# Products of constants in TensorE's waits, and a sparse attention whose side work is spread over more blocks

## The chip, the cores and the metric

The kernel runs on one core of a Trainium2 chip. The metric is the device time of one launch in microseconds (us). TensorE (PE) does the matrix products, VectorE (DVE) and ScalarE (ACT) the elementwise work, GpSimd (POOL) a few fills and loads, and SyncE issues most DMAs.

## The reference

The network has 256 tokens of width 1024, all in fp32. Two "hybrid" layers come first, then a pooling mixer with a gated network, then a sparse attention with a mixture of eight experts. Cut to what matters here:

```python
for layer in range(2):                      # hybrid layers
    h = rms_norm(x, norm1_g)
    mq, mk, mv, mo, mi, mf, aq, ak, av = split(h @ w_in)
    y = concat([mlstm(mq, mk, mv, mi, mf) * sigmoid(mo), dilated_attention(aq, ak, av)])
    x = x + y @ w_out
    x = x + relu(rms_norm(x, norm2_g) @ w_up) ** 2 @ w_down
x = rms_norm(x, final_g)
x = layer_norm(ALPHA * x + pool_mixer(x));  x = layer_norm(ALPHA * x + swiglu(x))
q, kc, vc, ks, vs, kw, vw, gates = split(x @ nsa_w_in)
kc, vc = compress(kc), compress(vc)         # silu(blocks @ w1) @ w2, 15 blocks of keys
o = g0 * attend(q, kc, vc) + g1 * attend(q, ks, vs) + g2 * attend(q, kw, vw)
x = layer_norm(ALPHA * x + o @ nsa_w_out);  x = layer_norm(ALPHA * x + moe_ffn(x))
```

## The kernel before

The tokens stand in two tiles of 128 rows. A weight matrix comes in units of 128 x 2048 through a ring of buffers. ScalarE copies each unit to `HI` in a rounded format (`split_hi`, L495), VectorE forms the rest `LO` (`split_lo`, L503), and TensorE makes every product of a weight as three products (L513), so that it keeps the precision of fp32. Activations are split in the same way after they are transposed: `turn_rows` (L671) transposes a tile of rows on TensorE into a PSUM bank, `cols_hi` (L678) and `cols_lo` (L686) write the two halves `XTH` and `XTL`, and only then can the products of that tile begin. `cols_by_tile` makes all products of tile 0 first, turns tile 1 between, and then makes those of tile 1.

Each engine runs one list of instructions in program order, and semaphores (`filled`, `a_bank`, `v_bank`, `a_done`, `v_done`) order them against one another. The `Banks` class deals out PSUM: four banks in turn with `take`, four named ones (`BA`) with `hold`. Whoever takes a bank waits until its last user's content has been read by ScalarE or VectorE.

In a hybrid layer `scores_tensor` (L1227) and `spread_sums_tensor` (L1214) belong to the mLSTM; `ml_turn_tensor` (L1238) and `ml_gather_tensor` (L1251) transpose its weights and multiply them by the values. The attention loops (`attention_tensor`, `attention_scalar`, `attention_vector`) run over blocks n of two heads: TensorE makes the scores of block n (`att_weigh`, L795), VectorE masks them and takes the maximum (L812, L816), ScalarE takes the exponential (L824), TensorE transposes the weights of block n-3 (`att_turn`, L833), ScalarE evicts them (L842), and TensorE multiplies those of block n-4 by the values (`att_gather`, L858). The dilated attention has 8 blocks, the sparse one 32 (two kinds of keys, two tiles, eight pairs of heads). `mid` is a table of extra steps: {n: work} runs that work in block n of the loop.

In the sparse attention the extra steps hold the whole branch of compressed keys: `blocks_tensor` (L1813) and `sparse_keys_tensor` (L1822) come before the loop; in the loop are `compress_tensor` (L1837) and `compress2_tensor` (L1850), the copy of the compressed values (`values_c_vector`, L2063), `weigh_c` (scores, softmax without its division: L1866, L2079 to L2088, ScalarE L2006), `turn_c` (division and transposition: L2093 to L2102, L1874, ScalarE L2011) and `gather_c` (product by the values and sum into `NY`: L1883, L2115, L2122). `sparse_heads` (L2129 to L2144) scales a finished tile of heads and adds it to `NY`.

`route_tensor` (L2274) counts the tokens of each expert, and `fetch_tensor` (L2295) gathers the rows of the first expert.

## Time and profile before

| | |
|---|---|
| median of 3 runs | 2351.45 us (2349.92 to 2353.35) |
| the profiled execution | 2355.53 us, of which the trace spans 2353.7 us |
| mean granted clock of TensorE | 0.958 of full speed |
| busy: TensorE, VectorE, ScalarE, GpSimd | 91%, 68%, 56%, 1% of the span |

The profile has one execution. A row of a timeline gives start and duration in us, the engine, the source line, what is written and read, the count, and in brackets how long the engine sat idle just before and whose instruction ended that wait.
### The profile page before, as it was taken

The page shows a single profiled execution, that of the slowest core. Times are in us where ns is not written, and L with a number is a line of the kernel's source. Part 1 is how long each engine was busy: PE and PEld are TensorE (multiplying, and loading weights), DVE is VectorE, ACT ScalarE, POOL GpSimd, SP SyncE. Part 2 cuts the span into 40 slices and gives each one's busy share as a digit, 9 for nine tenths or more (in the row PEclk, how much of TensorE's full clock was granted, in tenths as well). Part 3 has the DMA queues.
Part 4 walks back from the last instruction along what each step waited for, and adds up shares of the span by engine and source line. Part 5 has one row for each costly group of instructions (what it writes and reads, how often), then busy time and mean ns, then how long its engine had stood idle before and what let it go on. Part 6 is the DMA issues. An engine that isn't in the chain of part 4 may idle for free.

```text
span 2353.7 us, 25771 instructions
## 1 busy us (share of the span) xinstructions
PE 2137.2 (91%) x9918; PEld 1723.0 (73%) x9918; DVE 1596.9 (68%) x1540; ACT 1321.6 (56%) x1374; POOL 22.1 (1%) x33
## 2 busy tenths in 40 slices
PE   6888999978999799988777999999999989898986
PEld 5666887767788588777565888788888866666665
DVE  3865555775555554565655555788888889898997
ACT  4554444644444344445543444577776778787876
POOL 0000000000000000000000000000000000000000
PEclk9989999988999899997897999999999999999999
DMA  6313543431654254532005555688998999898995
GB/s 238 150 45 136 190 179 129 161 114 54 234 185 181 96 197 180 178 138 83 0 1 210 221 214 189 239 346 344 336 368 335 357 351 412 350 414 346 412 375 219
DMA packets 74336, 524.26 MB, mean 223 GB/s; under 512 B 8705, under 2 KB 9153, under 8 KB 11873
## 3 DMA queue, kind: packets, MB, share of 16 engines
q1 hardware_dynamic: 71424, 511.64, 56.7%
q0 software_dynamic: 2784, 10.93, 1.3%
q8 instruction: 80, 1.31, 0.2%
q14 instruction: 48, 0.39, 0.0%
HBM read 521.48 MB, written 1.05 MB: 222 GB/s over the span
## 4 chain that ended last, share of the span: by engine, by line
PE 71%; DVE 15%; ACT 8%; issue 5%; DMA 0%; DVEq 0%; ACTq 0%; SPq 0%
PE psum L513 52%; PE psum L523 8%; DVE LO L503 6%; ACT HI L495 3%; PE psum L1004 3%; DVE AR L1475 1%; PE psum L2295 1%; PE psum L1009 1%; PE psum L795 1%; PE psum L2323 1%; PE psum L858 1%; DVE XT L686 1%; ACT AR L824 1%; PE psum L671 1%; PE psum L1837 1%
## 5 line engine op out<-in xcount | busy, mean ns | idle before, releaser
L503 DVE TENSOR_TENSOR LO<-ring,HI 128x2048 fp32r<-128x2048 f32 x379 | 851.3, 2258 | 425.9 <-ACT HI L495 424.0
L495 ACT ACTIVATE HI<-ring 128x2048 fp32r<-128x2048 f32 x379 | 712.7, 1886 | 344.4 <-PE psum L513 282.5
L513 PE MATMUL psum<-HI,XT 128*128 128x512 f32 (+1 forms) x2592 | 842.4, 400 | 61.2 <-DVE XT L686 30.2
L513 PEld LDWEIGHTS psum<-HI,XT 128*128 128x128 f32 x2592 | 503.4, 195 | 178.8 <-DVE XT L686 34.2
L513 PE MATMUL psum<-LO,XT 128*128 128x512 f32 (+1 forms) x1296 | 514.3, 397 | 0.0
L513 PEld LDWEIGHTS psum<-LO,XT 128*128 128x128 f32 x1296 | 253.5, 196 | 50.5
L503 DVE TENSOR_TENSOR LO<-AR,HI 128x2048 fp32r<-128x2048 f32 x112 | 254.3, 2289 | 48.3 <-ACT HI L495 47.8
L523 PE MATMUL psum<-HI,XT 128*128 128x512 f32 x560 | 231.2, 413 | 39.8 <-DVE LO L503 38.4
L495 ACT ACTIVATE HI<-AR 128x2048 fp32r<-128x2048 f32 x112 | 213.4, 1911 | 61.7 <-PE psum L523 37.6
L513 PE MATMUL psum<-HI,HTH 128*128 128x512 f32 x568 | 225.1, 396 | 0.0
L513 PE MATMUL psum<-HI,HTL 128*128 128x512 f32 x568 | 221.6, 390 | 0.0
L513 PE MATMUL psum<-LO,HTH 128*128 128x512 f32 x568 | 221.2, 389 | 0.0
L523 PE MATMUL psum<-LO,XT 128*128 128x512 f32 x560 | 220.6, 394 | 0.0
L523 PEld LDWEIGHTS psum<-HI,XT 128*128 128x128 f32 x560 | 105.6, 188 | 99.4 <-issue 40.8
L967 ACT ACTIVATE AR<-psum 128x512 f32<-128x512 f32 (+1 forms) x107 | 63.5, 593 | 112.1 <-PE psum L513 93.1
L513 PEld LDWEIGHTS psum<-HI,HTL 128*128 128x128 f32 x568 | 106.6, 188 | 22.7
L513 PEld LDWEIGHTS psum<-LO,HTH 128*128 128x128 f32 x568 | 106.8, 188 | 21.0
L513 PEld LDWEIGHTS psum<-HI,HTH 128*128 128x128 f32 x568 | 106.7, 188 | 20.8
L523 PEld LDWEIGHTS psum<-LO,XT 128*128 128x128 f32 x560 | 105.8, 189 | 20.7 <-issue 1.0
L523 PE MATMUL psum<-HI,HTH 128*128 128x512 f32 x280 | 112.6, 402 | 5.0 <-DVE HTH L1061 4.6
L523 PE MATMUL psum<-LO,HTH 128*128 128x512 f32 x280 | 109.5, 391 | 0.0
L1025 ACT ACTIVATE HTH<-psum 128x512 fp32r<-128x512 f32 (+1 forms) x72 | 42.7, 593 | 57.4 <-PE psum L1009 52.8
(272 smaller groups left out, 1826.7 us busy)
## 6 DMA issues: line engine op xcount, KB each, us to landing
ring<-in_experts SPq DMA_DIRECT2D x224, 1024.0 KB, 6.8
ring<-in_dense SPq DMA_DIRECT2D x149, 1024.0 KB, 4.8
AR<-in_experts SPq DMA_DIRECT2D x112, 1024.0 KB, 6.8
bcs<-in_ln_g POOLq DMA_DIRECT2D x4, 512.0 KB, 4.5
bcs<-in_ln_b POOLq DMA_DIRECT2D x4, 512.0 KB, 5.0
bcs<-in_norm_g POOLq DMA_DIRECT2D x3, 512.0 KB, 4.0
cons<-in_cons POOLq DMA_DIRECT2D x1, 1317.0 KB, 8.1
X<-in_x SPq DMA_DIRECT2D x2, 512.0 KB, 4.1
```

Source lines behind the costliest of these rows:

```text
L495: e.activation(HI[:, h:h + m], slot(u), ACT.Copy).then_inc(*high.up(u))
L503: e.tensor_tensor(LO[:, h:h + m], slot(u), HI[:, h:h + m].bitcast(F32), ALU.subtract).then_inc(*low.up(u))
L513: ins = e.matmul(out_ap, lhsT=a, rhs=b, start=start and n == 0, stop=stop and n == m - 1)
L523: ins = e.matmul(out_ap, lhsT=both, rhs=b, start=start and n == 0, stop=stop and n == m - 1)
L671: ins = e.transpose(bank[:, j * P:(j + 1) * P], src(k0 + j), ident)
L686: e.tensor_tensor(XTL[:, k0:k0 + 4, tile(t)], banks.get(name, "cols", t, k0).rearrange("p (k s) -> p k s", k=4), XTH[:, k0:k0 + 4, tile(t) ...
L795: e.matmul(bank[:, 0:2 * nk], lhsT=a.qT[:, b, tile(qt)], rhs=a.kz(kind, b)[:, :, 0:nk], start=True, stop=True).then_inc(*filled.up(a.name, ...
L824: e.activation(w3[:, h, :], w3[:, h, :], ACT.Exp, bias=nm[:, h:h + 1], accum_out=l[:, 2 * b + h:2 * b + h + 1]).then_inc(*a_done.up(a.name ...
L858: ins = e.matmul(bank[:, col:col + 64], lhsT=a.PT2[:, n % 2, tile(h * kt + i)], rhs=a.v(kind, i, head), start=i == 0, stop=i == kt - 1)
L967: e.activation(GS[:, hb, t, 0:n], banks.get(use, "up", c, t)[:, 0:n], f).then_inc(*a_bank.up(use, "up", c, t))
L1004: ins = e.matmul(bank[:, o:o + PACK], lhsT=src[:, tile(j)], rhs=C("pairs"), start=True, stop=True)
L1025: e.activation(HTH[:, hb, 0:nb, tile(t)], bank[:, 0:n].rearrange("p (j s) -> p j s", j=nb), ACT.Copy).then_inc(*a_done.up(use, "turn", c, t))
```

## The change

A new function `idle` multiplies the identity matrix by 512 columns of constants, into the PSUM bank that is next in turn or a named one, and nobody reads the result. A bank that was last used so need not be waited for. There are 51 such products of 128x512, between the steps of TensorE's program: before or after transpositions (`wait`, `rest` of `turn_rows`), before `scores_tensor` and before the products of `av`, in blocks 2, 7 and 9 of the dilated attention, four at the start of the pooling, five between the transpositions of `blocks_tensor`, one before the queries of the sparse attention are transposed, and around the routing. `idle_first` makes 10, 18 and 4 products of 128x128 at the start of the first layer, when only the identity matrix is loaded. In the sparse attention the steps `turn_c`, `gather_c` and `weigh_c` of TensorE, ScalarE and VectorE move to later and different blocks; the sum over the weights (L2088) moves from `weigh_c` to the start of `turn_c`; the copy of the compressed values goes ahead of a `split_lo` in VectorE's list; the result of `compress2_tensor` goes to a named bank; and the turning and splitting of output tile 0 moves into the last blocks of the loop. The diff, cut to its core (ScalarE's table of steps changes in the same way: `weigh_c` to blocks 13 and 20, `turn_c` to 16 and 23):

```diff
     def hold(self, e, b, *use):
         before = self.use.get(b)
-        if before is not None:
+        if before is not None and before[0] != "idle":
...
+    def next(self, e, *use):
+        return self.hold(e, self.n % 4, *use)
...
-        def turn_rows(e, name, t, src, ready):
+        def idle(e, n, b=None):
+            if n:
+                bank = banks.next(e, "idle") if b is None else banks.hold(e, b, "idle")
+                e.wait_ge(s_cons, 16)
+                for _ in range(n):
+                    e.matmul(bank, lhsT=ident, rhs=cons[:, 0:512], start=True, stop=True)
+
+        def idle_first(e, n):
+            bank = banks.hold(e, BA[0], "idle")
+            e.wait_ge(s_ident, 16)
+            for _ in range(n):
+                e.matmul(bank[:, 0:P], lhsT=ident, rhs=ident, start=True, stop=True)
+
+        def turn_rows(e, name, t, src, ready, wait=0, rest=1, b=None):
+            idle(e, wait, b)
             for k0 in range(0, KB, 4):
...
+            idle(e, rest, b)
...
+            if l == 0:
+                idle_first(e, 10)
+            turn_rows(e, n1, 0, lambda k: ROWS[:, 0, tile(k)], rows_at(n1, 0), rest=l)
+            if l == 0:
+                idle_first(e, 18)
+            def second_rows():
+                turn_rows(e, n1, 1, lambda k: ROWS[:, 1, tile(k)], rows_at(n1, 1), wait=l, rest=l, b=BA[0])
+                if l == 0:
+                    idle_first(e, 4)
...
+            idle(e, 1)
             scores_tensor(e, l)
...
             spread_sums_tensor(e, l, 1)
+            idle(e, 1)
             cols(e, ("av", l), ("av", l), BOTH, xr, mid={0: lambda: ml_turn_tensor(e, l, 1),
...
-            attention_tensor(e, dilated(l), {1: lambda: ml_turn_tensor(e, l, 3),
-                                             2: lambda: ml_gather_tensor(e, l, 3)})
+            def gather_last():
+                idle(e, 1)
+                ml_gather_tensor(e, l, 3)
+            steps = {1: lambda: ml_turn_tensor(e, l, 3), 2: gather_last, 7: lambda: idle(e, 1),
+                     9: lambda: idle(e, 1)}
+            attention_tensor(e, dilated(l), steps)
...
         def pool_tensor(e):
+            idle(e, 4)
...
-            turn_rows(e, "l0", 0, lambda k: X[:, 0, tile(k)], [v_done.of("l0", "rows", 0)])
+            turn_rows(e, "l0", 0, lambda k: X[:, 0, tile(k)], [v_done.of("l0", "rows", 0)], wait=1,
+                      rest=3)
...
         def blocks_tensor(e, kind):
             for gp in range(2):
+                idle(e, 1 if kind or gp else 2)
...
-            bank = banks.take(e, "cmp", kind)
+            bank = banks.hold(e, BA[3 - kind], "cmp", kind)
...
-                     6: lambda: weigh_c_tensor(e, 0), 7: lambda: turn_c_tensor(e, 0),
-                     8: lambda: gather_c_tensor(e, 0), 9: lambda: weigh_c_tensor(e, 1),
-                     10: lambda: turn_c_tensor(e, 1), 11: lambda: gather_c_tensor(e, 1)}
-            attention_tensor(e, SPARSE, {2 * n: f for n, f in steps.items()})
+                     6: lambda: weigh_c_tensor(e, 0)}
+            steps = {2 * n: f for n, f in steps.items()}
+            steps |= {16: lambda: turn_c_tensor(e, 0), 18: lambda: gather_c_tensor(e, 0),
+                      19: lambda: weigh_c_tensor(e, 1), 23: lambda: turn_c_tensor(e, 1),
+                      25: lambda: gather_c_tensor(e, 1), 33: lambda: y_tile(0)}
...
-            y_tile(0)
+            attention_tensor(e, SPARSE, steps)
             project_out_tensor(e, ("po", 2), "out2", x_ready("y.2"), lambda: y_tile(1))
...
         def turn_c_vector(e, qt):
             l, gl, W = sm(16, "c_l"), sm(16, "c_gl"), WC[:, qt, :]
+            e.wait_ge(*a_done.of("wc", qt))
+            e.wait_ge(*v_order.last)
+            e.tensor_reduce(l, W.rearrange("p (h k) -> p h k", h=16), AX.X,
+                            ALU.add).then_inc(*v_done.up())
...
-                     4: lambda: hidden_vector(e, 1), 5: lambda: [split_lo(e), values_c_vector(e)],
+                     4: lambda: hidden_vector(e, 1), 5: lambda: [values_c_vector(e), split_lo(e)]}
...
+            steps |= {12: lambda: weigh_c_vector(e, 0), 14: lambda: turn_c_vector(e, 0),
+                      18: lambda: gather_c_vector(e, 0), 19: lambda: weigh_c_vector(e, 1),
+                      21: lambda: turn_c_vector(e, 1), 25: lambda: gather_c_vector(e, 1),
+                      34: lambda: cols_lo(e, "y.2", 0)}
...
         def route_tensor(e):
+            idle(e, 1)
...
-            turn_rows(e, "l2", 1, lambda k: X[:, 1, tile(k)], [v_done.of("l2", "rows", 1)])
+            turn_rows(e, "l2", 1, lambda k: X[:, 1, tile(k)], [v_done.of("l2", "rows", 1)], wait=4)
...
             route_tensor(e)
+            idle(e, 2)
```

How the lists of instructions change in three places. In the kernel of before, TensorE at the end of the dilated attention of layer 0 (from block 7's scores, L795, to the transposition of tile 0 of the output, L671):

```order
L795 MATMUL psum<-AR 128x512
L833 MATMUL psum<-cons,AR 128x128 x4
L858 MATMUL psum<-AR 128x64 x4
L833 MATMUL psum<-cons,AR 128x128 x4
L858 MATMUL psum<-AR 128x64 x4
L833 MATMUL psum<-cons,AR 128x128 x4
L858 MATMUL psum<-AR 128x64 x4
L833 MATMUL psum<-cons,AR 128x128 x4
L858 MATMUL psum<-AR 128x64 x8
L671 MATMUL psum<-cons,AR 128x128 x8
```

In the changed kernel, whose lines have moved (L818 is scores, L856 transposition, L881 the product by the values, L693 the output's transposition, L675 the product of constants):

```order
L818 MATMUL psum<-AR 128x512
L675 MATMUL psum<-cons 128x512
L856 MATMUL psum<-cons,AR 128x128 x4
L881 MATMUL psum<-AR 128x64 x4
L856 MATMUL psum<-cons,AR 128x128 x4
L881 MATMUL psum<-AR 128x64 x4
L675 MATMUL psum<-cons 128x512
L856 MATMUL psum<-cons,AR 128x128 x4
L881 MATMUL psum<-AR 128x64 x4
L856 MATMUL psum<-cons,AR 128x128 x4
L881 MATMUL psum<-AR 128x64 x8
L693 MATMUL psum<-cons,AR 128x128 x8
L675 MATMUL psum<-cons 128x512
```

Three products of constants stand in this stretch, two in the loop and one behind the output's transposition.

TensorE in blocks 14 to 18 of the sparse attention, before (L1874 is `turn_c`, L1883 `gather_c`):

```order
L795 MATMUL psum<-AR 128x512
L1874 MATMUL psum<-cons,AR 128x128 x4
L833 MATMUL psum<-cons,AR 128x128 x4
L858 MATMUL psum<-AR 128x64 x4
L795 MATMUL psum<-AR 128x512
L833 MATMUL psum<-cons,AR 128x128 x4
L858 MATMUL psum<-AR 128x64 x4
L795 MATMUL psum<-AR 128x256
L1883 MATMUL psum<-AR 128x256 x4
L833 MATMUL psum<-cons,AR 128x128 x4
L858 MATMUL psum<-AR 128x64 x4
L795 MATMUL psum<-AR 128x256
```

and in the changed kernel in blocks 16 to 19 (L1914 is `turn_c`, L1923 `gather_c`):

```order
L818 MATMUL psum<-AR 128x256
L1914 MATMUL psum<-cons,AR 128x128 x4
L856 MATMUL psum<-cons,AR 128x128 x4
L881 MATMUL psum<-AR 128x64 x4
L818 MATMUL psum<-AR 128x256
L856 MATMUL psum<-cons,AR 128x128 x4
L881 MATMUL psum<-AR 128x64 x4
L818 MATMUL psum<-AR 128x256
L1923 MATMUL psum<-AR 128x256 x4
L856 MATMUL psum<-cons,AR 128x128 x4
L881 MATMUL psum<-AR 128x64 x4
L818 MATMUL psum<-AR 128x256
```

`turn_c` stood in block 14 and stands in block 16; `gather_c` went from block 16 to block 18.

VectorE around `weigh_c` of tile 0, before (L2079 to L2088 is `weigh_c`, L2093 to L2102 `turn_c`):

```order
L2079 SCALAR_TENSOR_TENSOR AR<-psum,cons 128x512
L2083 TENSOR_REDUCE SML<-AR 128x16
L2085 TENSOR_TENSOR AR<-AR,SML 128x512
L2088 TENSOR_REDUCE SML<-AR 128x16
L812 SCALAR_TENSOR_TENSOR AR<-psum,cons 128x512
L816 TENSOR_REDUCE SML<-AR 128x2
L812 SCALAR_TENSOR_TENSOR AR<-psum,cons 128x512
L816 TENSOR_REDUCE SML<-AR 128x2
L2093 RECIPROCAL SML<-SML 128x16
L2096 SCALAR_TENSOR_TENSOR SML<-SML,cons,AR 128x16
L2102 COPY AR<-AR 128x4x4x32
```

and in the changed kernel (L2122 to L2128 is `weigh_c`, L2134 to L2146 `turn_c`, L835 and L839 the mask and maximum of a block):

```order
L2122 SCALAR_TENSOR_TENSOR AR<-psum,cons 128x512
L2126 TENSOR_REDUCE SML<-AR 128x16
L2128 TENSOR_TENSOR AR<-AR,SML 128x512
L835 SCALAR_TENSOR_TENSOR AR<-psum,cons 128x512
L839 TENSOR_REDUCE SML<-AR 128x2
L835 SCALAR_TENSOR_TENSOR AR<-psum,cons 128x512
L839 TENSOR_REDUCE SML<-AR 128x2
L2134 TENSOR_REDUCE SML<-AR 128x16
L2137 RECIPROCAL SML<-SML 128x16
L2140 SCALAR_TENSOR_TENSOR SML<-SML,cons,AR 128x16
L2146 COPY AR<-AR 128x4x4x32
```

The sum over the weights, which needs ScalarE's exponential, no longer follows directly behind the subtraction: two blocks' masks stand between.

## Rows read from the trace of the kernel before

**Rows 1.** The page: TensorE's granted clock in 40 slices

```profile
PEclk9989999988999899997897999999999999999999
```

**Rows 2.** Stretches of the span: length, busy us of PE, PEld, DVE, ACT, POOL, granted clock, DMA

```profile
0.00:1290.00 1290.00, 1136.58 (x5303) 928.55 (x5304) 739.08 (x983) 586.37 (x799) 22.13 (x33) 0.93 0.38 139
115.50:123.00 7.50, 5.59 (x14) 4.41 (x15) 5.29 (x9) 1.86 (x4) 0.00 (x0) 0.54 0.17 69
167.00:181.00 14.00, 12.54 (x48) 11.15 (x49) 4.20 (x8) 2.38 (x4) 0.44 (x1) 0.51 0.11 37
1075.00:1113.00 38.00, 33.54 (x141) 29.45 (x141) 19.45 (x48) 23.69 (x57) 0.00 (x0) 0.55 0.19 68
1127.20:1176.30 49.10, 37.18 (x205) 31.15 (x206) 34.51 (x69) 21.95 (x66) 0.00 (x0) 0.80 0.00 1
1235.00:1263.00 28.00, 15.11 (x73) 12.23 (x74) 13.01 (x43) 5.62 (x11) 2.80 (x3) 0.57 0.29 108
```

**Rows 3.** TensorE's timeline, tile 1 of the first projection

```profile
29.30 0.50 PE L513 MATMUL psum<-HI,XT 128*128 128x512 f32 x1 [1.77 <-DVE XT L686]
...
29.87 0.63 PE L513 MATMUL psum<-HI,XT 128*128 128x512 f32 x2
...
30.57 0.98 PE L513 MATMUL psum<-HI,XT 128*128 128x512 f32 x2
```

**Rows 4.** TensorE's timeline, one fp32 product of 128x512 at either clock

```profile
1138.07 2.02 PE L795 MATMUL psum<-AR 128*128 128x512 f32 x2
1139.88 0.65 PE L833 MATMUL psum<-cons,AR 128*128 128x128 f32 x4
...
1146.58 1.08 PE L795 MATMUL psum<-AR 128*128 128x512 f32 x2
1147.50 0.60 PE L833 MATMUL psum<-cons,AR 128*128 128x128 f32 x4
```

**Rows 5.** TensorE's timeline, from scores to spread sums, in layer 0 and 1

```profile
98.12 1.13 PE L1227 MATMUL psum<-AR 128*128 128x256 f32 x4 [1.31 <-DVE AR L908]
...
113.48 1.99 PE L1214 MATMUL psum<-AR,cons 8*128 8x256 f32 x8 [1.97 <-DVE AR L1568]
...
475.18 2.08 PE L1227 MATMUL psum<-AR 128*128 128x256 f32 x4 [1.31 <-DVE AR L908]
...
492.24 1.99 PE L1214 MATMUL psum<-AR,cons 8*128 8x256 f32 x8 [0.78 <-DVE AR L1568]
```

**Rows 6.** TensorE's timeline, waits at which the change puts something

```profile
18.43 0.77 PE L513 MATMUL psum<-HI,XT 128*128 128x512 f32 x1 [6.99 <-DVE LO L503]
...
117.41 0.77 PE L513 MATMUL psum<-HI,XT 128*128 128x512 f32 x1 [1.95 <-DVE AR L908]
...
166.95 1.80 PE L858 MATMUL psum<-AR 128*128 128x64 f32 x8 [2.53 <-ACT AR L842]
...
176.08 0.77 PE L513 MATMUL psum<-HI,XT 128*128 128x512 f32 x1 [1.46 <-DVE XT L686]
...
781.61 8.81 PE L1708 MATMUL psum<-AR,X 128*128 128x256 f32 x32 [5.93 <-DVE X L717]
...
1130.44 2.08 PE L795 MATMUL psum<-AR 128*128 128x512 f32 x2 [5.69 <-DVE AR L2063]
...
1144.81 0.66 PE L1874 MATMUL psum<-cons,AR 128*128 128x128 f32 x4 [2.53 <-DVE AR L2102]
...
1165.11 1.11 PE L1874 MATMUL psum<-cons,AR 128*128 128x128 f32 x4 [5.38 <-DVE AR L2102]
...
1204.14 0.47 PE L513 MATMUL psum<-HI,XT 128*128 128x512 f32 x1 [4.22 <-DVE XT L686]
...
1240.03 1.97 PE L671 MATMUL psum<-cons,X 128*128 128x128 f32 x8 [7.50 <-DVE X L752]
```

**Rows 7.** VectorE's timeline, first low half of the blocks, and copies of compressed values

```profile
1073.50 0.40 DVE L2034 TENSOR_TENSOR XT<-psum,XT 64x240 fp32r<-64x240 f32 x1 [1.31 <-ACT XT L1938]
...
1129.41 0.98 DVE L2063 COPY AR<-psum 32x64 f32<-32x64 f32 x4
```

39 lines of the change are left out of this document (17 added, 22 removed).

## The prediction

> **What bounds the kernel now.** I read the page first. TensorE is busy 91% of the span (table above), and the slices of its granted clock are not all 9: in the first half some are 8 and two are 7 [rows 1]. So I took the two halves of the span apart [rows 2]. Up to 1290 us the granted clock averages 0.93. The clock has two levels, 1.2 and 2.4 GHz, so a mean of 0.93 means that about 2 x 0.07 x 1290 = 180 us ran at the lower one. TensorE was busy in 1136.58 of those 1290 us, 88%, hence some 158 us of work ran at half speed, and no change of the clock alone can give back more than half of that, 79 us. The experts' half of the kernel (behind 1290 us) gets none of the change and is left at nothing.
>
> The timeline shows what the engine did before the clock fell. In tile 1 of the first projection TensorE turned a tile, then waited 1.77 us for VectorE's low half (L686), and soon its products come slower: a pair on `HI` takes 0.63 us at 29.87 and 0.98 at 30.57 [rows 3]. The same work at either level is in [rows 4]: the scores of a block of the sparse attention take 1139.88 - 1138.07 = 1.81 us from start to start at the low clock and 1147.50 - 1146.58 = 0.92 us at the full one. This is an fp32 product of 128x512, just what the change adds, so 0.92 and 1.81 us are the prices of one added product. A product of 128x128 I take at a quarter, 0.23 and 0.46 us (an estimate from the two).
>
> What one short stretch at the low clock costs is seen where both layers do the same work. From the wait before the third scores to the spread sums it takes 113.48 - 98.12 = 15.36 us in layer 0, where the clock stays up, and 492.24 - 475.18 = 17.06 us in layer 1, where it falls [rows 5]. So one such stretch costs 1.7 us, though waits on VectorE lie behind it.
>
> **Where the added products lie.** Each place must have a wait that covers 0.92 us. They are in [rows 6]: 6.99 us before the first product, 1.95 us before `av`, 2.53 us in the last blocks of the dilated attention, 1.46 and (elsewhere, as in rows 3) 1.77 us behind a turned tile, 5.93 us before the pooling, and 7.50 us before tile 1 of the experts' input. 51 products of 0.92 us are 47 us of work, and I cost what lies in these waits at nothing. The cover is gone where the product itself runs at the low clock: 1.81 us no longer fits in 1.77 or 1.46 us. The bank of an added product is the one that the next step takes, or one already read, so its wait is one that TensorE would have made anyway.
>
> **The terms.** (1) Dilated attention, both layers. The wait of 2.53 us before the product at 166.95 ends with ScalarE's L842, which the added products don't touch: the two of blocks 7 and 9, 1.84 us, fit in it. What follows at 167 to 181 us ran wholly at the low clock (0.51), with 12.54 us of busy TensorE [rows 2]; at full clock that is 6.3 us less. The wait for L686 at 176.08 stays and may grow by half a us, so 5.8 us, twice: 11.6.
> (2) Before `av`. The stretch 115.5 to 123 has 5.59 busy us at 0.54 [rows 2]; half is 2.8, of which I take 2.3, since a later wait on ScalarE takes some. Twice: 4.6.
> (3) Layer 1's scores: 1.7 [rows 5].
> (4) Tile 1 of five projections and networks, each with a stretch as in rows 3: 1.7 each, less where the next wait (on an eviction) takes some: 7.7.
> (5) Pooling: its products start at 781.61 behind 5.93 us of waiting [rows 6], where four added ones are 3.7 us; the network's first tile follows behind a like wait. A stretch each, the second with less work in it: 1.7 + 1.5 = 3.2.
> (6) Start: at 18.43 the first product records 0.77 us, as slow as the one at 176.08, against 0.50 us for a first product at full clock [rows 3, 6]. The start gains between nothing and one and a half stretches, 2.5 us; the ten products before the first transposition are 4.6 us at the low clock, begin only when the identity has landed, and may delay it by 1.1. I take 1.4.
> (7) Routing: 1235 to 1263 us is at a low clock, with 15.11 busy us [rows 2]. Half would be 7.5; the chain runs through many small VectorE steps and a DMA, so I take 4. Four products and one more lie in the 7.50 us of waiting.
> (8) Sparse attention. TensorE waits 5.69 us at 1130.44 behind the copies L2063, 2.53 at 1144.81 and 5.38 at 1165.11 behind `turn_c` of VectorE [rows 6]. With `turn_c` two blocks later on TensorE than on VectorE the last two should go. Of the first only the copy itself, 0.98 us [rows 7], goes, since VectorE's `split_lo` still waits for ScalarE's half of the unit. That is 2.53 + 5.38 + 0.98 = 8.9. Upper bound: in 1127.2 to 1176.3 VectorE is busy 34.51 of 49.10 us [rows 2], so 14.6 is all that there is before it becomes the bound; lower bound nothing, if the waits only move. At the end, the first product of the output waits 4.22 us (1204.14) behind VectorE's last heads and the splitting of tile 0 [rows 6]. With tile 0 turned and split inside the loop that wait nearly goes, 4.1, and the fall of the clock at 1204.7 with it, 1.7. Against that, two products (1.84 us) now stand ahead of the first transposition of `blocks_tensor`. ScalarE and then VectorE (L2034, which starts at 1073.50 behind ScalarE [rows 7]; its half of the tensors of one kind is eight such instructions) work their way from it to the first mask with hardly a pause, so this costs 1.4. Sum: 8.9 + 5.8 - 1.4 = 13.3. That the clock stays up in the compressing products, 1075 to 1113 us [rows 2], I do not assume: TensorE's waits on L2034 are longer than what is put into them.
>
> Two more places I cost at nothing. The product before the last gather of the mLSTM stands behind the wait that lets the clock fall, so it runs low (1.81 us, only partly covered) and may help the clock back. The one before the queries of the sparse attention is followed by a wait for ScalarE that takes it up.
>
> Sum: 11.6 + 4.6 + 1.7 + 7.7 + 3.2 + 1.4 + 4 + 13.3 = 47.5. Where the clock falls depends on moments that shift when everything before gets shorter, so some stretch will remain: I take off 4, which leaves 43.5 us. The profiled execution took 2355.5 us, 4 above the median of 2351.45; the differences are taken from the median: 2351.45 - 43.5 = 2308 us.
>
> **A rule of the Trainium skill.** At 29.30 us a wait of 1.77 us comes just before a fall of the clock [rows 3]. The Trainium skill, "TensorE: Matmul & The Clock Gate", in "Why this matters for your kernels", names only pauses clearly longer than that one as what makes the clock drop. By that rule terms 1 to 4 would give nothing; by the row they give. The trace speaks against the rule here.
>
> **Rivals.** A: only long waits matter, and filling the short ones changes nothing, as there something else pulls the clock down, for instance the transpositions around them. Then terms 1 to 4 go and 5 to 8 stay: 3.2 + 1.4 + 4 + 13.3 = 21.9, or 2329.5 us. For it: the stretch at 1075 us is low with TensorE 88% busy [rows 2], so more than waiting counts. Against it: rows 3 and 5. The rule above would end here too. Chance 0.15.
> B: the clock holds, but the spreading of the sparse attention gives nothing, since VectorE has as much to do and its two long pieces (`gather_c`, heads) now meet around block 19. Then 13.3 becomes -1.4: 47.5 - 14.7 - 4 = 28.8, or 2322.6 us. For it: VectorE is at 70% there. Chance 0.15.
> C: the clock also holds through the compressing products: 33.54 busy us at 0.55 are up to 15 us more, of which 12: 2296 us. Chance 0.10.
> D, slower: the clock doesn't respond, and the products run low. Of the 51, some 25 stand ahead of a step that another engine waits for (scores, last gather, dilated attention, blocks, pooling, routing); at 1.81 us each that is 45 us, of which waits cover about half, so 23 us are added against 10 from the spreading: 2351.45 + 13 = 2364 us. It decides once uncovered time is more than what clock and spreading give back. Rows 3 speak against it. Chance 0.05.
> E: gains and costs cancel, within 0.2%: 0.03.
>
> **How the numbers follow.** The forecast has 0.52, with 2299 to 2317 as its own range. The range of all reaches down to 2290, past C, and up to 2332, past A and B; D and the far ends are outside, under 0.2 together. 0.2% of the time is about what a measurement of this kernel can tell from no change. Every case but D and E is faster: 0.92, same 0.03, slower 0.05.
>
> **What would show each step.** The mean clock up to 1290 us should rise from 0.93 to about 0.97. In the two stretches behind the dilated attention it should be near 1 and the wait before L842's reader about 0.7 us instead of 2.53 (1). Layer 1 should take the same 15.4 us as layer 0 (3). The product behind the sparse attention should wait under 1 us instead of 4.22, and TensorE's waits behind `turn_c` be gone (8); if VectorE's idle time in the loop stays while TensorE waits on its masks instead, B is right. `blocks_tensor` should finish some 3.5 us later on TensorE, and L2034 start 1.4 us later. What would make me wrong above all: a clock that falls at new places as often as it stays up at the old ones.

## The result, and the profile after

The changed kernel takes 2323.91 us, the median of 4 runs (2321.12 to 2327.8), against 2351.09 us of the kernel before (4 runs): the ratio is 0.9883, with a 95% interval of 0.9869 to 0.9897. 27.2 us were gained where 43.5 were forecast. The time lies in the whole range (2290 to 2332), but outside the forecast's own 2299 to 2317; of the cases priced it is nearest to rival B's 2322.6, whose mechanism (the spreading gives nothing) the runs below refute. The profiled execution spans 2326.0 us, 27.7 less than the 2353.7 us of before.

The page of the changed kernel (busy us, share of the span and instructions; granted clock in 40 slices):

```profile
PE 2166.2 (93%) x10084; PEld 1729.2 (74%) x10084; DVE 1597.3 (69%) x1540; ACT 1322.1 (57%) x1374; POOL 22.2 (1%) x33
...
PEclk9989999999999999997898999999999999999999
```

TensorE is busy 29.0 us more than before, though the span is 27.7 us shorter: it waits less, and what fills the waits is no work of the network. Of the four 8s that [rows 1] has in its first sixteen slices three have become 9s; around the middle the 7s and 8s are still there but for one 7.

Stretches of the changed kernel (columns as in [rows 2]); the first and the last answer to the first and the fourth of [rows 2]:

```profile
0.00:1261.00 1261.00, 1163.66 (x5470) 932.88 (x5471) 739.32 (x983) 586.85 (x799) 22.20 (x33) 0.96 0.38 143
111.00:118.00 7.00, 7.00 (x16) 4.41 (x15) 6.48 (x12) 0.02 (x1) 0.00 (x0) 0.51 0.36 143
163.00:173.00 10.00, 8.98 (x42) 7.49 (x43) 5.23 (x9) 3.26 (x6) 0.54 (x1) 0.66 0.14 54
1066.00:1098.00 32.00, 29.47 (x130) 26.74 (x129) 15.27 (x37) 19.77 (x46) 0.00 (x0) 0.57 0.19 67
```

Up to the experts the granted clock is 0.96 where it was 0.93; 2 x 0.04 x 1261 = 101 us ran at the lower level, against some 180. The compressing products (1066 to 1098) still run low for 2 x 0.43 x 32 = 28 us, where 2 x 0.45 x 38 = 34 us were low before. The places at 111 and at 163 us, ahead of `av` and at the end of the dilated attention, are still low too, though products of constants stand in both.

To see where the 27.7 us came from, the start of the same VectorE instruction was read in the timelines of both profiles; how much the distance to the start above it has shrunk is what that stretch gained. The starts, and the terms of the prediction (in us):

```
the stretch ends at (in brackets the term)     before    changed  gained  forecast
splitting of tile 1, first projection (6)        27.76     26.28    1.48    1.4
after tile 1 of that projection (4)              39.12     36.03    1.61
dilated attention, past av, last gather (2)     154.47    151.54   -0.16    2.3
end of the dilated attention (1)                185.12    178.97    3.22    5.8
after tile 1 of layer 0's network (4)           416.19    408.77    1.27
layer 1's scores (3)                            491.49    482.40    1.67    1.7
dilated attention, past av, last gather (2)     533.31    524.03    0.19    2.3
end of the dilated attention (1)                563.94    551.43    3.23    5.8
two projections' tile 1 (4)                     604.77    589.02    3.24
pooling, tile 1 of its network (5)              814.14    800.61   -2.22    3.2
tile 1 of the queries (4; 7.7 for its five)    1019.63   1004.45    1.65    7.7
blocks of the compressed keys, L2034 (8)       1073.50   1059.65   -1.33   -1.4
mask behind the copies L2063 (8)               1130.49   1114.54    2.10    1.0
loop, to the last heads (8)                    1199.08   1179.67    3.46    7.9
tail, to the output's tile 1 (8)               1212.58   1187.76    5.41    5.8
routing and first gather (7)                   1276.56   1246.44    5.30    4.0
end of the span                                2353.7    2326.0    -2.42    0
taken off for stretches that remain                                        -4
sum                                                                27.70   43.5
```

Terms 3, 4, 6, the blocks and the tail fit within half a us. That is a fit of one profile to one profile; which of these gains are the products' is read below, in two more. At the scores of layer 1 the distance of [rows 5] is now 483.14 - 467.78 = 15.36 us, what layer 0 had (TensorE's timeline):

```profile
467.78 1.13 PE L1250 MATMUL psum<-AR 128*128 128x256 f32 x4 [1.31 <-DVE AR L931]
...
483.14 3.31 PE L1237 MATMUL psum<-AR,cons 8*128 8x256 f32 x7 [1.94 <-DVE AR L1605]
```

The misses are four: term 1, term 2, term 5 and the loop in term 8.

### The profile page after: what moved, and what is told of

Same layout as the page of the kernel before. It is cut to its first block, busy times and chain, and to the rows that moved or that the text cites. A ratio compares the mean times of both kernels' runs of the same rounds, so it can differ in the third digit from the quotient of the medians.

```text
span 2326.0 us, 26094 instructions
## 1 busy us (share of the span) xinstructions
PE 2166.2 (93%) x10084; PEld 1729.2 (74%) x10084; DVE 1597.3 (69%) x1540; ACT 1322.1 (57%) x1374; POOL 22.2 (1%) x33
## 3 DMA queue, kind: packets, MB, share of 16 engines
HBM read 521.48 MB, written 1.05 MB: 225 GB/s over the span
## 4 chain that ended last, share of the span: by engine, by line
PE 72%; DVE 15%; ACT 8%; issue 5%; DMA 0%; DVEq 0%; ACTq 0%; POOLq 0%
PE psum L517 51%; PE psum L527 9%; DVE LO L507 6%; ACT HI L499 3%; PE psum L1027 3%; DVE AR L1512 1%; PE psum L1032 1%; PE psum L2340 1%; PE psum L2368 1%; PE psum L675 1%; PE psum L881 1%; PE psum L818 1%; DVE XT L709 1%; ACT AR L847 1%; PE psum L1877 1%
## 5 line engine op out<-in xcount | busy, mean ns | idle before, releaser
L517 PE MATMUL psum<-HI,XT 128*128 128x512 f32 (+1 forms) x2592 | 828.6, 394 | 33.5 <-DVE XT L709 11.8
L517 PEld LDWEIGHTS psum<-HI,XT 128*128 128x128 f32 x2592 | 493.0, 191 | 156.7 <-DVE XT L709 24.5
L517 PE MATMUL psum<-LO,XT 128*128 128x512 f32 (+1 forms) x1296 | 505.8, 390 | 0.0
L527 PEld LDWEIGHTS psum<-HI,XT 128*128 128x128 f32 x560 | 106.6, 190 | 98.1 <-issue 40.3
```

The lines of the kernel that those rows point to most:

```text
L517: ins = e.matmul(out_ap, lhsT=a, rhs=b, start=start and n == 0, stop=stop and n == m - 1)
L527: ins = e.matmul(out_ap, lhsT=both, rhs=b, start=start and n == 0, stop=stop and n == m - 1)
```

## The experiments

The times are medians of 4 to 6 runs (one run for `changed_again`), and each median has its ratio to runs of the kernel before on the same chip. A ratio is uncertain by 0.12 to 0.23%, 3 to 5 us, so what is smaller is read in the profiles; and a profile is one execution, whose stretches at the low clock are its own.

**The two halves of the change.** `constants_only` has all products of constants and the old tables of steps; `spread_only` has the new tables and in `idle` and `idle_first` no product.

> This kernel has all the products of constants, and the sparse attention as it was before (steps in the old blocks, output tile 0 transposed behind the loop). Theory: constants and spreading act apart. In the two profiles VectorE's instructions of the sparse attention's loop gain 4.4 us and the turning of the output's tile 0 another 5.4 us, some 10 of the 27 us; the rest, 17 us, is the constants', so about 2334 us. Rival: the spreading's gain comes mostly from the clock that the constants hold, and alone the constants give more: 2328 us or less. Second rival: the spreading is most of the change, as the constants' own cost eats their gain: 2342 us or more.

> This kernel has the sparse attention as in the changed kernel and no product of constants. Theory: spreading gives 10 us, so about 2341 us, and its stretches at the low clock ahead of the sparse attention are those of the kernel before. Rival (the two need each other): no faster than 2346 us, since the clock falls in the loop where TensorE waits. The other side: the spreading alone gives 15 us or more (2336 us), as forecast from the waits behind the steps (8.9 and 5.8 us).

Measured: 2333.82 us (0.9927, 0.9913 to 0.9940) and 2340.59 us (0.9955, 0.9942 to 0.9969). Against 2351.0 these are gains of 17.2 and 10.4 us, 27.6 together, where the whole change gives 27.2. Within what these medians can tell the halves act apart, and the first theory holds in both runs; rival B (the spreading gives nothing) is out.

**Are the short waits worth anything?**

```diff
-        def turn_rows(e, name, t, src, ready, wait=0, rest=1, b=None):
+        def turn_rows(e, name, t, src, ready, wait=0, rest=0, b=None):
...
-            idle(e, 1)
             scores_tensor(e, l)
...
-             7: lambda: idle(e, 1), 9: lambda: idle(e, 1)}
```

> The changed kernel without 30 of the 51 products of constants and without the last four of the start: those around every transposed tile of rows, before the scores, before the product of av, before the last gather and in blocks 7 and 9 of the dilated attention, where TensorE waits 2.6 us at most. Those in long waits (pooling, blocks, routing, start) and the spread sparse attention stay. Theory: the short waits are worth most of what the constants give: 7.8 us at tile 1 of five places, 6.5 us at the ends of the dilated attention, 1.7 us at layer 1's scores, 16 us, so about 2340 us. Rival A of the prediction (only long waits matter): 2324 us, no change.

Measured: 2339.34 us (0.9955, 0.9942 to 0.9969), 15.4 us slower than the changed kernel. Rival A (only long waits matter) is out. The end of the dilated attention is again what it was in [rows 6], waits and slow product alike (TensorE's timeline of this kernel):

```profile
163.74 1.93 PE L881 MATMUL psum<-AR 128*128 128x64 f32 x8 [2.53 <-ACT AR L865]
...
173.00 0.77 PE L517 MATMUL psum<-HI,XT 128*128 128x512 f32 x1 [1.46 <-DVE XT L709]
```

**One kernel, two profiles.** The changed kernel was profiled once more.

> The changed kernel once more, for a second profile of the same instructions. Theory: which stretches run at the low clock differs from one execution to the next, so the ends of the two dilated attentions, which ran low for 6.8 us each in the first profile and for none in that of the kernel with the constants alone, may be low or not; the span lies between 2318 and 2327 us. Rival: the low stretches are fixed by the program, and stand at the same instructions as in the first profile.

Measured: 2324.05 us, span 2322.2. Stretches of the second profile, the ends of both dilated attentions:

```profile
165.50:172.50 7.00, 7.00 (x33) 6.70 (x33) 2.92 (x6) 1.59 (x3) 0.00 (x0) 0.51 0.22 75
535.00:548.00 13.00, 10.45 (x63) 8.44 (x62) 6.56 (x11) 4.62 (x8) 0.00 (x0) 1.00 0.01 2
```

and the second end in the first profile:

```profile
537.00:545.50 8.50, 8.50 (x40) 7.08 (x40) 3.86 (x7) 1.94 (x4) 0.00 (x0) 0.60 0.00 1
```

Layer 0's end is low in both; layer 1's was at 0.60 in the first and is at 1.00 in the second. The theory holds: the same instructions run at either level from one execution to the next. Over the ten profiles of kernels with these products, 14 of the 20 ends are low for 6.8 us and 6 not at all. In the three kernels without them there (before, `spread_only`, `no_short_waits`) all six ends are low for 13.7 us.

The starts that gave the table of gains were read in this second profile too, and in that of `spread_only`, which up to the sparse attention has the instructions of the kernel before and no product of constants. Gains against the profile of before, in us:

```
the stretch ends at                     changed   changed again   spread_only
splitting of tile 1, first projection      1.48        0.40           0.60
after tile 1 of that projection            1.61        1.60           1.62
layer 0: past av, last gather             -0.16        0.12          -1.24
layer 0: end of the dilated attention      3.22        2.65           0.02
after tile 1 of layer 0's network          1.27        1.32          -1.58
layer 1's scores                           1.67        1.17           1.67
layer 1: past av, last gather              0.19        1.12          -0.01
layer 1: end of the dilated attention      3.23        5.31           0.00
two projections' tile 1                    3.24        3.23           3.23
pooling, tile 1 of its network            -2.22        0.37           0.10
tile 1 of the queries                      1.65        1.59          -0.03
```

Two things follow. One place's gain differs by up to 2.6 us between two executions of the same kernel (pooling). And at three places `spread_only` gains as much without any product: 1.62 in the first projection, 1.67 at layer 1's scores, 3.23 at layer 1's two projections, 6.5 us in all. `no_short_waits` agrees, with no product ahead of the scores and 488.89 - 473.54 = 15.35 us from them to the sums:

```profile
473.54 1.13 PE L1250 MATMUL psum<-AR 128*128 128x256 f32 x4 [1.31 <-DVE AR L931]
...
488.89 1.99 PE L1237 MATMUL psum<-AR,cons 8*128 8x256 f32 x8 [1.94 <-DVE AR L1599]
```

A stretch of `spread_only` over the two projections:

```profile
560.00:610.00 50.00, 42.51 (x194) 33.93 (x193) 28.93 (x30) 23.52 (x27) 3.01 (x5) 1.00 0.58 209
```

So the profile of before had low stretches there that other executions without the products don't have, and its 6.5 us aren't shown to be the products' gain. What the two profiles do show as theirs is tile 1 of layer 0's network (2.9 us against `spread_only`), tile 1 of the queries (1.6 to 1.7) and the ends of the dilated attention (2.6 to 3.2 us where they run low, 5.3 where they don't).

**A bank that isn't empty: the pooling.** The place where the changed kernel lost in its first profile. Its TensorE, from the products ahead of the pooling to the network's first:

```profile
759.78 3.59 PE L675 MATMUL psum<-cons 128*128 128x512 f32 x8
...
765.88 8.83 PE L1746 MATMUL psum<-AR,X 128*128 128x256 f32 x32 [2.50 <-DVE X L740]
...
784.95 1.09 PE L693 MATMUL psum<-cons,X 128*128 128x128 f32 x8 [1.41 <-DVE X L775]
...
788.61 5.42 PE L675 MATMUL psum<-cons 128*128 128x512 f32 x6 [2.57 <-DVE AR L1795]
...
793.11 1.15 PE L517 MATMUL psum<-HI,XT 128*128 128x512 f32 x1
```

The same first product in the kernel before:

```profile
805.95 0.77 PE L513 MATMUL psum<-HI,XT 128*128 128x512 f32 x1 [4.14 <-DVE AR L1756]
```

and VectorE in the changed kernel, the reading of the pooled tile 1:

```profile
787.86 0.69 DVE L1795 TENSOR_TENSOR AR<-psum,AR 128x512 f32<-128x512 f32 x1
```

The three products behind the transposition (L675, x6) could start at 786.0, but wait 2.57 us for L1795, since the bank next in turn holds the pooled tile 1. They then run at the low clock, and the network's first product comes at 793.11: 27.23 us behind the first pooling product, where before it was 805.95 - 781.61 = 24.34 [rows 6].

```diff
-            turn_rows(e, "l0", 0, ..., wait=1, rest=3)
+            turn_rows(e, "l0", 0, ..., wait=1, rest=3, b=BA[0])
```

> The changed kernel, but the four products of constants around the pooled tile 0 are written to a named bank that is empty instead of the bank next in turn. Theory: in the changed kernel the three behind the transposition wait for VectorE's read of the pooled tile 1 (they start at 788.6 us, 2.57 us late) and then run at the low clock, so that the network's first product starts 3 us after its own bank came free; in the empty bank they start as soon as the transposition ends, and that product starts 2.5 to 3.5 us earlier, 2321 us in all. Rival: the bank is not what holds it, the product waits for VectorE's chain as in the kernel before, and the change of bank moves the start of the first product by less than 1 us.

```profile
764.13 8.83 PE L1746 MATMUL psum<-AR,X 128*128 128x256 f32 x32 [2.50 <-DVE X L740]
...
784.19 2.74 PE L675 MATMUL psum<-cons 128*128 128x512 f32 x6
...
788.50 0.47 PE L517 MATMUL psum<-HI,XT 128*128 128x512 f32 x1 [1.57 <-DVE AR L1795]
```

Now the three start at 784.19 as soon as the transposition ends, and the first product comes 788.50 - 764.13 = 24.37 us behind the pooling's: the 2.9 us are back, and the stretch at the low clock in the network (787 to 794 us) is gone as well. From VectorE's reading of the pooled tile 1 (L1795) to its next splitting (L709) it takes 3.6 us less. The theory holds. The median, 2323.29 us (0.9882, 0.9867 to 0.9898), hardly shows it; the profiled execution is the fastest of the four (2319.24).

The clock has a part in the 2.9 us. The changed kernel's second profile has the same wait of 2.57 us:

```profile
764.69 7.14 PE L1746 MATMUL psum<-AR,X 128*128 128x256 f32 x32 [2.50 <-DVE X L740]
...
785.73 4.52 PE L675 MATMUL psum<-cons 128*128 128x512 f32 x6 [2.57 <-DVE AR L1795]
```

but its first pooling products take 7.14 us where they took 8.83, and the network's first product comes 789.27 - 764.69 = 24.58 us behind them. With the 1.69 us of the pooling products set aside, the wrong bank costs 24.58 - (24.37 - 1.69) = 1.9 us there, and 2.9 in the first profile. Of the nine profiles with the bank next in turn four have 27.2 us, one 26.1 and four 24.5 to 24.7.

**Ahead of `av`.** In the first profile of the changed kernel the clock falls just behind the wait ahead of layer 0's spread sums (at 111.2 us), before the added product is reached, so that it runs low itself (TensorE's timeline):

```profile
110.41 3.07 PE L1237 MATMUL psum<-AR,cons 8*128 8x256 f32 x8 [1.94 <-DVE AR L1605]
...
113.41 2.08 PE L675 MATMUL psum<-cons 128*128 128x512 f32 x2
```

Two kernels put one product more ahead of the sums:

```diff
+            idle(e, 1)             # av_before_sums: bank next in turn
+            idle(e, 1, BA[0])      # av_empty_bank: a bank read long before
             spread_sums_tensor(e, l, 1)
             idle(e, 1)
```

> The changed kernel with one product of constants more in each layer, ahead of the spread sums of the second pair of heads, where TensorE waits 1.94 us. Theory: the clock falls there because of the wait ahead of the sums, and the product that the change has put behind the sums comes too late; with one in that wait too, the stretch at the low clock at 111 to 118 us goes in both layers, and this place gains 1.5 to 2.5 us each, 2320 us in all. Rival (the clock isn't ruled by single waits): a low stretch of the same length stays within 10 us of the place, and the time stays at 2324 us or grows by the uncovered part, about 1 us.

Measured: 2337.63 us (0.9937, 0.9923 to 0.9950), 13.7 us slower than the changed kernel. Neither theory nor rival had that. The profile shows the larger part of why: the bank next in turn is still read by L931, so the product waits 3.38 us where the sums waited 1.94, and the sums begin at 114.07 and no longer at 110.41:

```profile
112.06 2.07 PE L675 MATMUL psum<-cons 128*128 128x512 f32 x2 [3.38 <-DVE AR L931]
...
114.07 3.78 PE L1237 MATMUL psum<-AR,cons 8*128 8x256 f32 x8
```

By VectorE's starts the two places lose 3.9 and 2.7 of the 9.9 us by which this profile is longer than the changed kernel's first. Another 2.6 go at the tail of the sparse attention, where the clock falls at 1186.7 us; no run shows what brings that about.

> As the earlier run with a product ahead of the spread sums, but into a named bank that has been read long before (in the earlier run the product waited 3.38 us for a bank that VectorE's L931 read, where the sums alone waited 1.94 us). Theory: now it lies in the wait, the clock stays up at 111 to 118 us, and each layer gains 1 to 2 us: 2321 us. Rival: the clock falls there for other reasons (the small sums and transpositions around it), and the time stays within 1.5 us of 2324 us.

```profile
113.64 1.02 PE L675 MATMUL psum<-cons 128*128 128x512 f32 x2
...
114.60 1.99 PE L1237 MATMUL psum<-AR,cons 8*128 8x256 f32 x8
...
116.51 1.13 PE L675 MATMUL psum<-cons 128*128 128x512 f32 x2
...
118.48 0.50 PE L517 MATMUL psum<-HI,XT 128*128 128x512 f32 x1 [0.84 <-DVE AR L931]
```

Measured: 2320.18 us (0.9865, 0.9850 to 0.9880), 3.7 us below the changed kernel, with intervals that overlap. In this layer there is no wait ahead of the product or the sums, all run at the full clock, and the first product of `av` takes 0.50 us. But here an earlier low stretch (96.8 to 103.6 us) had made TensorE late. In layer 1 of the same profile a wait of 1.08 us is left, and the clock falls for 3.4 us behind the sums:

```profile
481.82 1.99 PE L1237 MATMUL psum<-AR,cons 8*128 8x256 f32 x8 [1.08 <-DVE AR L1606]
```

In the three profiles with this product (here, `three_banks`, `block9_twice`) the stretch past `av` gains 1.4 to 1.6 us in layer 0, where the seven of kernels with the other products and without this one gain -0.2 to 0.2. In layer 1 the scores and the stretch past `av` together gain 2.2 us in all three and 1.9 to 3.2 in the seven, so nothing is shown there. The product in the read bank is worth about 1.6 us, then, and the rest of the 3.7 isn't shown to be its own; in the wrong bank it costs 13.7.

**The end of the sparse attention.** Of the loop and the tail, VectorE and TensorE of the changed kernel:

```profile
1138.79 0.69 DVE L2122 SCALAR_TENSOR_TENSOR AR<-psum,cons 128x512 f32<-128x512 f32 x1
...
1141.54 1.42 DVE L2181 TENSOR_TENSOR AR<-psum,SML 128x512 f32<-128x512 f32 x2
...
1143.06 0.42 DVE L835 SCALAR_TENSOR_TENSOR AR<-psum,cons 128x256 f32<-128x256 f32 x1
...
1180.17 0.69 DVE L2181 TENSOR_TENSOR AR<-psum,SML 128x512 f32<-128x512 f32 x1
```

```profile
1143.54 0.70 PE L818 MATMUL psum<-AR 128*128 128x256 f32 x2 [2.07 <-DVE AR L835]
...
1146.18 1.11 PE L881 MATMUL psum<-AR 128*128 128x64 f32 x4 [1.73 <-ACT AR L865]
...
1180.92 0.50 PE L517 MATMUL psum<-HI,XT 128*128 128x512 f32 x1 [2.34 <-DVE AR L2181]
```

In block 19 the subtraction (L2122, with two more to 1140.93) and the heads (L2181) stand one behind the other, and the mask behind them comes at 1143.06, for which TensorE waits 2.07 us. At the tail the first output product begins with the end of L2181, which reads the bank of tile 1: `cols_by_tile` claims both tiles' banks before it makes the products of either. Two kernels try these two places.

> The changed kernel, but the bank of the output's tile 1 is claimed behind the products of tile 0 and not ahead of them, and tile 0 of the output is transposed two blocks sooner, copied by ScalarE inside the loop and split by VectorE one block sooner. Theory: in the changed kernel the output's first product waits 2.34 us and ends its wait with VectorE's L2181 of the last heads, which frees the bank of tile 1, not its own; then it starts right behind the attention's last product, 2 us earlier, 2322 us. Rival: the wait moves to tile 1, whose heads and splitting are as late as before, and nothing is gained by the start of the next stage.

Measured: 2326.7 us (0.9891, 0.9877 to 0.9906), with runs from 2320.98 to 2330.64, not faster. The transposition of tile 0, two blocks sooner, takes a bank in turn that VectorE's splitting (L712 in its numbers) frees late. The attention's own transposition waits for it, and the clock falls with it:

```profile
1174.80 1.12 PE L859 MATMUL psum<-cons,AR 128*128 128x128 f32 x4 [1.96 <-DVE XT L712]
...
1175.70 1.81 PE L884 MATMUL psum<-AR 128*128 128x64 f32 x8
...
1181.43 0.77 PE L517 MATMUL psum<-HI,XT 128*128 128x512 f32 x1
```

The wait ahead of the first output product is gone, but it begins at 1181.43 and not sooner. Neither theory nor rival had the late bank.

The other kernel moves the steps of tile 1 (TensorE's table; those of the other two engines move likewise):

```diff
-         19: weigh_c_tensor(e, 1), 23: turn_c_tensor(e, 1), 25: gather_c_tensor(e, 1)
+         20: weigh_c_tensor(e, 1), 24: turn_c_tensor(e, 1), 26: gather_c_tensor(e, 1)
```

> The changed kernel, with the steps of the compressed keys' tile 1 one block later on every engine (scores 19 to 20, exponential 20 to 21, division 21 to 22, transposition 23 to 24, product by the values 25 to 26). Theory (rival B of the prediction in part): in block 19 VectorE has the scores' subtraction and maximum (2.1 us) and the heads of tile 1 (2.0 us) one behind the other, TensorE waits 2.07 us for the mask L835 behind them and 1.73 us for ScalarE after that, and the clock falls; with a block between them both waits shrink and the loop gains 2 to 4 us, 2321 us. Rival: VectorE's work in the loop is the bound, the waits only move to other blocks, and the time stays within 1 us of 2324 us.

```profile
1143.28 0.44 PE L856 MATMUL psum<-cons,AR 128*128 128x128 f32 x2 [0.44 <-DVE AR L835]
...
1149.15 0.66 PE L881 MATMUL psum<-AR 128*128 128x64 f32 x4 [1.73 <-ACT AR L865]
...
1154.89 1.12 PE L818 MATMUL psum<-AR 128*128 128x512 f32 x2 [1.30 <-ACT AR L2053]
```

Measured: 2330.43 us (0.9905, 0.9889 to 0.9921), and the runs reach from 2322.07 to 2333.72. The wait of 2.07 us is down to 0.44 and two of about half a us, and the clock stays up around it, as expected. But the 1.73 us behind ScalarE is unchanged, a new wait of 1.30 us for its copy L2053 stands at 1154.89, and the clock falls at 1167 and 1185 us, where it had held. The theory falls in its size and sign. In VectorE's masks the loop is 1.2 us ahead of the changed kernel's up to 1167 us, and gives back 1.8 behind the fall at 1167.9; the tail loses 1.6 more behind that at 1185, and 2.0 of the profile's 4.6 us were lost at the kernel's start, which is the same in both. So the move itself gains a little, and whether the falls follow from it or from the moment stays open.

**The compressing products.**

```diff
                 for n, (a, b_) in enumerate(...):
                     ins = e.matmul(bank[:, 0:62], ...)
+                if r % 4 == 1:
+                    idle(e, 1, BA[3 - kind])
```

> The changed kernel with eight products of constants more, one behind every fourth part of the compressing products (L1877). In the changed kernel TensorE is at the low clock for 27.3 us from 1066 us on, though it is busy in 26.8 of them. Theory: the compressing products themselves hold the clock down, not waits, since they are many and small; larger products between them bring it back for part of the stretch: 7 us or more of the low time go, which pays for about half of the 7.4 us that are added, and the time is 2324 to 2328 us. Rival C of the prediction (waits hold it down): the fillers change nothing at the clock and cost 10 us or more, 2334 us.

```profile
1061.00:1089.00 28.00, 26.98 (x91) 21.10 (x91) 11.42 (x23) 14.43 (x33) 0.00 (x0) 0.51 0.11 38
1089.00:1110.00 21.00, 18.32 (x112) 13.31 (x110) 11.98 (x27) 12.05 (x32) 0.00 (x0) 1.00 0.16 53
```

Measured: 2338.3 us (0.9951, 0.9932 to 0.9970), with runs from 2329.67 to 2344.79; the profile is that of the fastest. The clock is low from 1061 to 1089 us with TensorE busy 26.98 of 28 us, then high: in sum as much low time as the 27 us of the changed kernel, in one piece. So the fillers took nothing away: VectorE is 6.8 us later behind this stretch, about the 7.4 us of the eight products, and the theory's 7 us are not there. The median's 14.4 us are more than that; where the rest goes isn't known. Clock and time came out as the rival had them. That waits hold the clock down here, as rival C had it, isn't supported either, with TensorE busy 96%. The cause stays open.

**What adds up.** `three_banks` has the pooling's and the sums' empty banks, and claims the bank of tile 1 behind tile 0's products:

```diff
             for t in range(nt):
-                banks.hold(e, at[t], *use, t) if at else banks.take(e, *use, t)
+                if at is None:
+                    banks.take(e, *use, t)
             us = next_units(e, (*key, 0), n)
             for t in range(nt):
+                if at:
+                    banks.hold(e, at[t], *use, t)
```

> The changed kernel with three repairs of what a product waits for: the products at the pooled tile in an empty bank, one product more in an empty bank ahead of the spread sums, and the bank of the output's tile 1 claimed only behind tile 0's products. Theory: the gains add, 3 at the pooling in the profile, 3.7 in the median at the sums, 1.2 at the output, 6 to 8 us in all: 2317 us. Rival: a stretch at the low clock that is cleared at one place comes back at another, and the sum is worth no more than the best of them, 2320 us.

Measured: 2315.63 us (0.9847, 0.9834 to 0.9859), 8.3 us below the changed kernel, with all five runs between 2312.8 and 2315.69. The gains add: 8.3 us, where the figures forecast for the single repairs (3, 3.7 and 1.2) make 7.9. In the profile they are 3.6 us at the pooling, 1.8 past `av` of layer 0 and 1.3 at the output, whose first product waits 1.05 us for its own tile's splitting, where it waited 2.34 us; another 2 us come from layer 0's end of the dilated attention, which ran at the full clock without a repair.

**The wait that was left.** At the end of the dilated attention (TensorE, changed kernel) the product of block 9 stands right before the wait, but 1.59 us of it are left; the prediction had 0.7:

```profile
160.91 1.08 PE L675 MATMUL psum<-cons 128*128 128x512 f32 x2
...
164.02 1.10 PE L881 MATMUL psum<-AR 128*128 128x64 f32 x8 [1.59 <-ACT AR L865]
...
171.74 0.77 PE L517 MATMUL psum<-HI,XT 128*128 128x512 f32 x1
```

> The kernel with the three repairs (2315.6 us in its run), and in block 9 of both dilated attentions two products of constants instead of one. In all profiles of kernels with the products a wait of 1.59 us for ScalarE's L865 is left there, and the clock falls behind it at some ends and not at others (14 of 20 ends ran low for 6.8 us). Theory: the second product takes that wait to 0.7 us and the clock stays up at both ends in most executions, which is worth 3.2 us an end where it ran low: about 4 us, 2312 us. Rival: whether the clock falls there isn't decided by the 0.9 us; the end of one layer still runs low in the profile and the time stays within 1.5 us of 2315.6 us.

```profile
531.36 1.94 PE L678 MATMUL psum<-cons 128*128 128x512 f32 x4
...
534.46 1.10 PE L884 MATMUL psum<-AR 128*128 128x64 f32 x8 [0.73 <-ACT AR L868]
...
540.45 0.50 PE L517 MATMUL psum<-HI,XT 128*128 128x512 f32 x1 [0.91 <-DVE XT L712]
```

Both ends now run at full clock, 0.73 us of the wait are left, and from block 9's products to the output's first one layer 1 takes 540.45 - 531.36 = 9.09 us, with one product more, where `three_banks` had 10.51. The median is 2313.76 us (0.9833, 0.9810 to 0.9856), 1.9 below `three_banks`, within what the intervals allow for no change: three runs lie at 2310.5 to 2313.8 and two at 2322.3 and 2324.4. The profiled one is the former of those two, and shows where it loses. Its compressing products, and those of `three_banks` (the same instructions):

```profile
1058.00:1104.00 46.00, 43.23 (x182) 37.35 (x181) 22.61 (x48) 27.22 (x64) 0.00 (x0) 0.55 0.14 47
```

```profile
1058.00:1104.00 46.00, 42.00 (x210) 35.20 (x209) 24.16 (x53) 30.75 (x71) 0.00 (x0) 0.70 0.14 47
```

The clock is 0.55 against 0.70 over 46 us, 14 us more at the low level; that and what follows up to the first mask is 3.8 of the 7.6 us by which this profile is longer, and 2.1 more lie at the kernel's start. Both ends and the 0.7 us came out as expected; the median it should have moved is spread by other places. That two good ends are typical isn't shown by one profile, as layer 0's end ran at the full clock in that of `three_banks` too.

## Why the prediction was right, and what was mis-sized

**The bound and the mechanism** were right in the main. The clock answers to short waits: without the products in them 15.4 us go, and the clock up to the experts rose to 0.96 (0.97 was named). The sum was 16 us too high, as four terms fell short together, and the range held the time because it was wide enough to take in rivals A and B.

**What fitted, in part by luck.** Terms 3, 4, 6 and the cost of the blocks came out to a tenth, term 7 gave 1.3 more. But the sign that was named for term 3, layer 1 taking layer 0's 15.4 us, came true in `no_short_waits` as well, without the product. It and 4.9 of the 7.8 us of term 4 are as large in `spread_only`: they were low stretches of the one profile of before, which took 4 us more than the median. Term 6 (1.4, measured 1.48) lies between -1.0 and 2.7 us in the eleven profiles with the changed start, and term 7 between 4.6 and 6.9 in those that leave its place and the tail before it as they are.

**The rule** of the Trainium skill that the prediction weighed ("TensorE: Matmul & The Clock Gate", "Why this matters for your kernels") names only clearly longer pauses; `no_short_waits`, whose unfilled waits are 2.6 us at most, decides against it here. Another section of that page of the Trainium skill, "A second HAM failure mode: psum-queue depth-cycling", has a kernel whose clock goes up and down because of frequent short pauses at bank changes. By that section the short waits count, and the run agrees.

**Term 1** (11.6, measured 6.5). The step that failed is "the two of blocks 7 and 9, 1.84 us, fit in it": only block 9's product stands in the wait, so 1.59 us are left and not 0.7, and behind 1.59 us the clock falls in 14 of 20 ends. In the six ends where it held, the stretch gained 5.3 us against the 5.8 forecast. So the size was near for the good case, and the forecast took that case for the rule. The section "What's actually happening" of the same page of the Trainium skill says that the number of slow products at the start differs between executions of one kernel; the trace shows the like in mid-kernel.

**Term 2** (4.6, measured 0; 1.2 in the second profile). The stretch 115.5 to 123 was counted as if a product behind the sums could keep it away. In the first profile the clock falls at the wait before the sums, one step earlier, which the prediction didn't look at. In layer 0 of the second it falls behind the added product, at 114.3 us, so one product there isn't enough either. With the wait before the sums filled too, layer 0 gets 1.4 to 1.6 us, and the stretch is shorter, not gone.

**Term 5** (3.2, measured -2.2; 0.4 in the second profile). Two steps failed. Four products did not fill the wait ahead of the pooling: 2.50 us of it are left, and in the first profile the clock falls behind it all the same, in the second it holds. The other is "The bank of an added product is the one that the next step takes, or one already read, so its wait is one that TensorE would have made anyway". At the pooled tile the next step waits for that bank too, but three products at the low clock then stand between the bank and the step. `pool_bank` moves them to an empty one and has the 2.9 us back, of which 1.9 remain where the clock is alike.

**Term 8** (13.3, measured 9.6). Its tail and its cost were right. In the loop all 7.9 us of waits behind `turn_c` were counted as gone; they are, but behind its first mask there are now 2.60 us of waits for masks and 4.47 us for ScalarE's evictions (before 0.23 and 1.87), and the loop gained 3.5. That is half of what rival B described. Ahead of the loop the place behind the copies gave 2.1 us for 1.0. `weigh_later` shows that taking away the largest of the new waits by moving steps isn't enough. This term is the spreading's: `constants_only` gains nothing in the loop (-0.04) or at the tail (0.01).

**The 4 us taken off** for stretches that remain were 2.4, in the experts, whose products are the same. In the other profiles that part of the kernel lies between -2.6 and 0.5 us; no run looked into it.

**The rivals.** A and B are out by their runs, D (slower) by the result. C gave nothing: the clock doesn't hold in the compressing products.

## What to carry to other kernels

Filling a wait of TensorE pays only if the filler waits for nothing itself: look up who last reads its bank, since the same product cost 13.7 us in one bank and gained about 1.6 in another. Look for the first wait before a fall of the clock and fill that one; a filler behind it runs low itself. Where a clock that depends on the moment is at work, read several executions, of the kernel before above all, before a single one's stretches are priced: a low stretch that is gone in the new profile may be gone in the next one of the old kernel too.

## What the runs showed of the hardware

The same instructions run at 1.2 or at 2.4 GHz in different executions of one kernel (layer 1's end: 0.60 and 1.00), and the times of one kernel spread by up to 15 us with its mean clock (`block9_twice`: 0.983 in the run of 2310.48 us, 0.973 in that of 2324.42; `compress_filled`: 0.977 at 2329.67, 0.968 at 2344.79). And in `compress_filled` TensorE is recorded busy in 26.98 of 28 us, the compressing products with constants between them, at a granted clock of 0.51. The only waits over half a us near it end before the clock falls or as it does (1.48 us at 1059.96 and 1.18 at 1061.79, ahead of L1862), and what holds the clock down behind them isn't known.
